# A gated DeltaNet whose triangular solve on GpSimd goes from 16x16 to 32x32 blocks

## What is computed

```python
    decay = jnp.exp(jnp.where(lower, g[..., :, None] - g[..., None, :], -jnp.inf))
    a = jnp.where(strict, jnp.einsum('nbhcd,nbhsd->nbhcs', k_beta, k) * decay, 0.0)
    eye = jnp.eye(DN_CHUNK, dtype=q.dtype)
    t_inv = lax.linalg.triangular_solve(a + eye, jnp.broadcast_to(eye, a.shape),
                                        left_side=True, lower=True, unit_diagonal=True)
    u = jnp.einsum('nbhcs,nbhsd->nbhcd', t_inv, v * beta[..., None])
    w = jnp.einsum('nbhcs,nbhsd->nbhcd', t_inv, k_beta * jnp.exp(g)[..., None])
    ...
        v_new = u_c - jnp.einsum('bhcd,bhde->bhce', w_c, state)
        o_c = (jnp.einsum('bhcd,bhde->bhce', q_c * jnp.exp(g_c)[..., None], state)
               + jnp.einsum('bhcs,bhse->bhce', qk_c, v_new))
    ...
    o = _rmsnorm_f32(o, norm_w) * jax.nn.silu(z.astype(jnp.float32).reshape(bsz, seqlen, DN_NV, DN_DV))
    return o.reshape(bsz, seqlen, DN_V_DIM).astype(x.dtype) @ w_out
```

## Time and profile before

| what | us |
|---|---|
| three runs, median (lowest to highest) | 1464.47 (1462.7 to 1466.74) |
| the profiled execution | 1463.22 |
| its span on the core | 1461.4 |
| TensorE busy in it | 1374.9 (94%), 7494 matmul records |
| VectorE, ScalarE, GpSimd busy | 782.5, 364.7, 293.9 |
| mean granted TensorE clock | 0.978 |

### The profile page before, as it was taken

How to read it: one execution, slowest core, us unless ns; L and a number is a source line. 1 busy time by engine, 2 the same in 40 slices (tenths; PEclk the granted TensorE clock), 3 DMA queues, 4 the chain that set the end, 5 groups by cost and what they waited for, 6 DMA issues and landing times. The chain is left out here.

```text
span 1461.4 us, 21006 instructions
## 1 busy us (share of the span) xinstructions
PE 1374.9 (94%) x7494; PEld 823.8 (56%) x7494; DVE 782.5 (54%) x1577; ACT 364.7 (25%) x788; POOL 293.9 (20%) x529
## 2 busy tenths in 40 slices
PE   8899699999999999999899899999999999889996
PEld 5468268576685766857686433336544544533332
DVE  2765465756657566575556543247344544835227
ACT  3322122222222222222222122102332232222110
POOL 2240613325133251332401200021000000200011
PEclk9999899999999999999899999999999999999998
DMA  7367321313213132122524599981021118299983
GB/s 211 112 179 218 89 74 30 102 38 91 67 37 97 34 97 61 41 68 90 140 76 145 187 387 399 399 314 42 23 75 39 41 39 311 107 349 399 399 311 127
DMA packets 173251, 220.90 MB, mean 151 GB/s; under 512 B 57280, under 2 KB 107840, under 8 KB 173184
## 3 DMA queue, kind: packets, MB, share of 16 engines
q1 hardware_dynamic: 141664, 173.65, 35.6%
q10 hardware_dynamic: 26432, 28.32, 5.7%
q0 software_dynamic: 5088, 18.02, 3.4%
HBM read 185.62 MB, written 34.34 MB: 151 GB/s over the span
## 5 line engine op out<-in xcount | busy, mean ns | idle before, releaser
L498 PE MATMUL bank<-xT,wgu 128*128 128x512 f32 x448 | 195.3, 595 | 0.0
L1894 PE MATMUL bank<-wgu,moe_xgT 128*32 128x512 f32 x1536 | 169.8, 594 | 4.3 <-issue 3.9
L498 PEld LDWEIGHTS bank<-xT,wgu 128*128 128x128 f32 x448 | 84.6, 191 | 101.5 <-issue 101.5
L546 PE MATMUL bank<-wd,oT 128*128 128x512 f32 x256 | 122.1, 614 | 1.4 <-issue 1.4
L590 PE MATMUL bank<-wd,xT 128*128 128x256 f32 x512 | 119.8, 380 | 0.0
L1145 DVE SCALAR_TENSOR_TENSOR wgu<-bank,taps,wgu 128x510 f32<-128x510 f32 (+1 forms) x128 | 95.5, 746 | 44.7 <-ACT wgu L785 38.6
L1894 PEld LDWEIGHTS bank<-wgu,moe_xgT 128*32 128x32 f32 x1536 | 50.1, 110 | 105.8 <-issue 95.0
L590 PEld LDWEIGHTS bank<-wd,xT 128*128 128x128 f32 x512 | 95.0, 191 | 11.4
L1917 PE MATMUL bank<-wd,moe_hidT 128*32 128x512 f32 x768 | 87.1, 593 | 7.2 <-issue 4.1
L2161 DVE TENSOR_TENSOR moe_hid<-moe_silu,bank 128x256 f32<-128x256 f32 x24 | 10.1, 421 | 129.7 <-ACT moe_silu L2004 129.7
L546 PEld LDWEIGHTS bank<-wd,oT 128*128 128x128 f32 x256 | 46.9, 197 | 45.7 <-issue 44.7
(11 more groups left out here) (354 smaller groups left out, 2407.0 us busy)
## 6 DMA issues: line engine op xcount, KB each, us to landing
wgu<-moe_w_gate SPq DMA_DIRECT2D x32, 1024.0 KB, 14.3
wgu<-moe_w_up SPq DMA_DIRECT2D x32, 1024.0 KB, 15.6
wd<-moe_w_down SPq DMA_DIRECT2D x32, 1024.0 KB, 15.4
wgu<-dn_w_in SPq DMA_DIRECT2D x32, 512.0 KB, 4.1
slots_x<-gains SPq DMA_DIRECT2D x1, 9984.0 KB, 35.6
wd<-dn_w_in SPq DMA_DIRECT2D x8, 1024.0 KB, 6.0
wd<-dn_w_out ACTq DMA_DIRECT2D x16, 512.0 KB, 4.4
xT<-slots_x ACTq DMA_DIRECT2D x16, 512.0 KB, 8.6
```

Source lines behind the costliest of these rows:

```text
L498: mm = pe.matmul(bank[:], wqkv[:, ct, k], xT[:, k], start=k == 0, stop=k == KD - 1)
L546: mm = pe.matmul(ps[uses.at[f"{name}{n}"][0]][:], oT[:, h, tt], wo[:, h, half * 512:(half + 1) * 512], start=h == 0, stop=h == 1)
L1894: mm = pe.matmul(ps[2][seats].rearrange("p (a f) -> p a f", a=2), xgT[:, j % ROW_BUFS, k, seats], wgu[:, e % RING, :, k], start=k == 0, st ...
```

## The change

BASE becomes 5: GpSimd inverts blocks of 32 x 32, and levels 5 and 6 are left. Each block lies on two partitions: both have all of the scaled block N, and each has one half of the columns of T. The loop goes over k from 31 to 1. The straight and turned results go out with three stores (T_kept counts 48), the unturned halves in rows of 16 numbers. `take_blocks` has four stores and four loads, `place_solved` and `place_half` two DMAs each. The output scales stand in the middle of the solve (`midway`, behind k = 16). ScalarE clears `forms` in its window, so GpSimd has no memsets in the loop. On TensorE two output products (six in the last head) stand ahead of the first level. VectorE's fourth convolution stands in the window with the others. SP issues the loads of beta, and the zero fill stands behind the blocks of head 1.

```diff
-LEVELS, BASE = 7, 4
+LEVELS, BASE = 7, 5
...
-OUTPUT_EARLY, OUTPUT_LATE = [(f"y{n}", 0) for n in range(4)], [(f"y{n}", n % 2) for n in range(4, 8)]
+OUTPUT_EARLY, OUTPUT_LATE = [("y0", 0), ("y1", 2), ("y2", 0), ("y3", 1)], [(f"y{n}", n % 2) for n in range(4, 8)]
...
-        scaled = sb("scaled", [P, BLK, BLK])
-        raw_blk, S = sb("raw_blk", [P, BLK, BLK]), sb("S", [P, BLK, BLK])
-        prod = sb("prod", [P, 64])
-        T_blk = sb("T_blk", [P, 2, BLK, BLK])
+        HALF = BLK // 2
+        raw_blk = X.rearrange("p c t n -> p (c t n)").rearrange("p (r c) -> p r c", r=BLK)
+        N = W.rearrange("p c t n -> p (c t n)").rearrange("p (r c) -> p r c", r=BLK)
+        T = sb("T", [P, BLK, HALF])
+        T_turned = sb("T_turned", [P, HALF, BLK])
+        prod = sb("prod", [P, HALF * HALF])
...
                 for d in range(2):
-                    sp.dma_start(raw_blk[d * 64:d * 64 + 64].rearrange("p r c -> p (r c)"), t["A_rows"]).then_inc(blocks_in, 16)
+                    for half in range(2):
+                        sp.dma_start(raw_blk[d * 64 + half:d * 64 + 64:2].rearrange("p r c -> p (r c)"), t["A_rows"]).then_inc(blocks_in, 16)
 
             def place_solved(n):
 
                 sp.wait_ge(T_solved, n + 1)
-                sp.dma_start(t["T_rows"].rearrange("f q n -> q f n"), T_blk[:].rearrange("p f r c -> p f (r c)")).then_inc(T_kept, 16)
-                sp.wait_ge(T_kept, (n + 1) * 16)
+                sp.dma_start(t["T_rows"][0], T_turned[:].rearrange("p c r -> p (c r)")).then_inc(T_kept, 16)
+                by_half = t["T_rows"][1].rearrange("(q a) (r c) -> q (a r c)", a=2, c=BLK).rearrange("q (r a c) -> a q r c", a=2, c=HALF)
+                for half in range(2):
+                    sp.dma_start(by_half[half], T[half:P:2]).then_inc(T_kept, 16)
+                sp.wait_ge(T_kept, (n + 1) * 48)
                 sp.wait_ge(forms_zero, n + 1)
                 for b in range(P // BLK // 2):
                     place_blocks(sp, b)
...
             load_w(1, True)
             load_spans(1)
             solve_blocks(0)
-            sp.wait_ge(zeroed, 1)
-            sp.dma_start(t["router_w"], dram["router_w"].rearrange("(k p) e -> p k e", p=P)).then_inc(t["router_in"], 16)
-            sp.dma_start(t["router_b"][:], dram["router_bias"].partition_broadcast(P)).then_inc(t["router_in"], 16)
-
-            for rows, n in ((t["slots_x"], BLOCKS), (t["slots_y"][FETCHED * P:], 1)):
-                blocks = rows.rearrange("(b p) n -> p b n", p=CAP)
-                sp.dma_start(blocks, zeros.rearrange("p (a n) -> p a n", a=1).to_broadcast([CAP, n, D])).then_inc(zero_filled, 16)
             load_w(2, True)
             load_spans(2)
             solve_blocks(1)
             load_z(1, True)
+            sp.wait_ge(zeroed, 1)
+            sp.dma_start(t["router_w"], dram["router_w"].rearrange("(k p) e -> p k e", p=P)).then_inc(t["router_in"], 16)
+            sp.dma_start(t["router_b"][:], dram["router_bias"].partition_broadcast(P)).then_inc(t["router_in"], 16)
+            for rows, n in ((t["slots_x"], BLOCKS), (t["slots_y"][FETCHED * P:], 1)):
+                blocks = rows.rearrange("(b p) n -> p b n", p=CAP)
+                sp.dma_start(blocks, zeros.rearrange("p (a n) -> p a n", a=1).to_broadcast([CAP, n, D])).then_inc(zero_filled, 16)
...
-                if not following:
+                if following:
+                    filler(2)
+                else:
                     pe.wait_ge(cols_in, 64)
                     pe.wait_ge(*last_read(uses, 2, i))
                     pe.matmul(ps[2][:, 0:4 * KD], cols[:], ident[0:4 * KD, 0:4 * KD], start=True, stop=True).then_inc(cols_turned, 1)
-                    filler(4)
+                    filler(6)
...
-                act.wait_ge(T_kept, (n + 1) * 16)
+                act.wait_ge(T_kept, (n + 1) * 48)
                 act.wait_ge(forms_zero, n + 1)
                 for b in range(P // BLK // 2, P // BLK):
                     place_blocks(act, b)
+
+            def clear_forms(f):
+                act.wait_ge(rows_in, 16)
+                for d in range(2):
+                    ins = act.copy(forms[:, f, d].rearrange("p h t n -> p (h t n)"), zero_col.to_broadcast([P, 8 * P]))
+                if f:
+                    ins.then_inc(forms_zero, 1)
...
             def window(uses, i, n):
                 middle_tap(uses, i, n, 0)
+                if uses is not FIRST_HEAD:
+                    clear_forms(0)
                 for ct in range(1, 4):
                     middle_tap(uses, i, n, ct)
                     act_silu(n, ct - 1)
+                    if ct == 1 and uses is not FIRST_HEAD:
+                        clear_forms(1)
                     if ct == 2:
                         place_half(n - 1)
...
+                pool.wait_ge(blocks_in, (i + 1) * 64)
                 for d in range(2):
                     some = slice(64 * d, 64 * (d + 1))
                     raw = raw_blk[some].rearrange("p r c -> p c r") if d else raw_blk[some]
-                    step(nc.gpsimd.tensor_tensor(S[some], raw, scaled[some], ALU.mult))
-                step(nc.gpsimd.tensor_tensor(S[:].rearrange("p r c -> p (r c)")[:, 0:BLK * BLK:BLK + 1], ones[:, 0:BLK], ones[:, 0:BLK], ALU.mult))
-                for k in range(BLK - 2, 0, -1):
-                    n = BLK - 1 - k
+                    step(nc.gpsimd.tensor_tensor(N[some], raw, over_cols[some], ALU.mult))
+                for k in range(BLK - 1, 0, -1):
+                    lo = max(0, k - HALF)
+                    n = HALF - lo
                     part = prod[:, 0:k * n].rearrange("p (r c) -> p r c", r=k)
-                    step(nc.gpsimd.tensor_tensor(part, S[:, 0:k, k:k + 1].to_broadcast([P, k, n]), S[:, k:k + 1, k + 1:].to_broadcast([P, k, n]), ALU.mult))
-                    step(nc.gpsimd.tensor_tensor(S[:, 0:k, k + 1:], S[:, 0:k, k + 1:], part, ALU.add))
-                nc.gpsimd.tensor_tensor(T_blk[:, 1], S[:], over_cols, ALU.mult)
-                nc.gpsimd.tensor_tensor(T_blk[:, 0], S[:].rearrange("p r c -> p c r"), over_rows, ALU.mult).then_inc(T_solved, 1)
+                    step(nc.gpsimd.tensor_tensor(part, N[:, 0:k, k:k + 1].to_broadcast([P, k, n]), T[:, k:k + 1, lo:].to_broadcast([P, k, n]), ALU.mult))
+                    step(nc.gpsimd.tensor_tensor(T[:, 0:k, lo:], T[:, 0:k, lo:], part, ALU.subtract))
+                    if k == HALF:
+                        midway()
+                step(nc.gpsimd.tensor_tensor(T_turned[:], T[:].rearrange("p r c -> p c r"), over_turned, ALU.mult))
+                nc.gpsimd.tensor_tensor(T[:], T[:], over_rows, ALU.mult).then_inc(T_solved, 1)
...
+                def output_scales():
+                    for n in range(2):
+                        pool.wait_ge(oss_ready, 1 + i * 2 + n + 1)
+                        rsqrt(nc, t, pool, rs[:, 4 * n:4 * n + 4], ss[:, 4 * n:4 * n + 4], C_EPS_O, rs_added, i * 2 + n + 1).then_inc(rs_ready, 1)
+
                 if following:
                     key_scales(i + 1)
-                    solve(i + 1)
-                for n in range(2):
-                    pool.wait_ge(oss_ready, 1 + i * 2 + n + 1)
-                    rsqrt(nc, t, pool, rs[:, 4 * n:4 * n + 4], ss[:, 4 * n:4 * n + 4], C_EPS_O, rs_added, i * 2 + n + 1).then_inc(rs_ready, 1)
-                if following:
-                    clear_forms()
+                    solve(i + 1, output_scales)
+                    pool.wait_ge(o_step, 1 + (i + 1) * 8)
                     decayed_scores(i + 1)
+                else:
+                    output_scales()
...
-                for ct in range(3):
...
-                    for slot, job in enumerate(taps_apart(None, i, i + 1, 3)):
-                        jobs[slot] = [job]
-                    jobs[4] = [lambda: silu(i + 1, 2)]
-                    jobs[8] = [lambda: silu(i + 1, 3)]
+                    jobs[2] = [lambda: silu(i + 1, 3)]
                 if earlier:
-                    for n, slot in enumerate((3, 5, 7, 9)):
-                        jobs.setdefault(slot, []).append(lambda n=n: add_output("y", n if following else 4 + n))
+                    for n, slot in zip((1, 0, 2, 3), (0, 1, 4, 5)) if following else ((6, 4), (7, 5)):
+                        jobs.setdefault(slot, []).append(lambda n=n: add_output("y", n))
                 if not following:
-                    jobs["window"] = [lambda: weight_rows()] + [lambda n=n: add_output("y", n) for n in range(4)]
+                    jobs["window"] = [lambda: weight_rows()] + [lambda n=n: add_output("y", n) for n in range(6)]
```

More of the change, by code:

```diff
@@ L41 @@
 C_ROW = C_HALF + 40
-C_SEAT = C_ROW + BLK * BLK
+C_SEAT = C_ROW + 2 * 16
 CAP = 96
@@ L411, in _ @@
             load_z(0, False)
+            sp.wait_ge(beta_kept, 16)
+            for h in range(2):
+                for d in range(2):
+                    by_block = t["beta_rows"][d * NV:(d + 1) * NV].rearrange("(n h) (b j) -> h b n j", h=2, j=BLK)
+                    for half in range(2):
```

(40 more changed lines are left out.)

21 lines of the change are left out of this document (10 added, 11 removed).

## The result

The changed kernel takes 1550.7 us (median of four runs, 1547.9 to 1557.0). The kernel before took 1463.6 on the same chip: the ratio is 1.0582, 95% interval 1.0551 to 1.0614. The profiled execution has a span of 1547.9 us and a mean granted clock of 0.942; before it was 1461.4 and 0.978. The prediction was 1520, 1482 to 1558, slower. Its sign, its range and its mechanism held, and its value was 31 us short.

A forecast was written before the change was run, and what follows sets the result against it. TensorE bounds the kernel before; after the change the blocks' path, 68.4 us against 62.9 of cover, sets the head. Accumulated X delays reach +64 at head 7, less 7.3 behind it: +57 on 1463.2 gives 1520 us, range 1482 to 1558.

The forecast's parts named there:

- Head 0's X product: First X product of head 0 at 123.8 us against 91.62, +32.2, with nothing to cover the longer solve.
- Heads 3 to 6: Steady heads: 92.5 us each, 1.6 more than before.
- the ways out: From solved blocks to X product: 5.6 us to store T and 5.2 us to load forms.
- I add 1.0 us: Second half of GpSimd's solve: VectorE's scans running beside it lengthen it by 1.0 us.
- Head 1 to head 2, the fill: Zero fill delays head 2's blocks to 63.2 us after its issue; head 2's X product at 328.4 us, +47.0.
- Head 6 to head 7: Head 7, with no projections behind its scores: 89.8 us behind head 6, against 79.29 before.
- The cover: Steady head: the blocks' path of 68.4 us exceeds its cover of 62.9, so the X product waits about 5.5 us.
- The first rival: Solve stays under cover through less GpSimd time per element; TensorE remains the bound and the kernel ends faster; 5%.
- The second: Rival: solve 4 to 7 us shorter than taken, heads 3 to 6 at about 85.6 us, kernel 1464 to 1480; 7%.
- the third: Rival: the small stores of T pace the path, 8 us more in each of eight heads, kernel 1586 us; 6%.
- at no cost: ScalarE's clears of forms, the fourth convolution in the window and the beta loads on SP were claimed to add no time.
- The clock's 1.5 us a head: TensorE's low clock behind each pause ahead of the levels: 1.5 us a head, between 0 and 2.9.

The follow-up runs named there:

- experiment 5: Changed kernel with the zero fill issued under head 0's solve and VectorE's four scans moved behind the masks of the scores: 1508.3 us, 1.0277 of the kernel before.
- experiment 2: Changed kernel with the router loads and zero fill issued while head 0 is being solved: 1525.2 us, 1.0416 of the kernel before.
- experiment 1: Changed kernel with GpSimd's loop stopped behind k = 16, so T is not the inverse: 1516.0 us, 1.0347 of the kernel before.
- experiment 4: Changed kernel with the unturned halves of T stored as whole 2 KB rows, not 64 byte pieces: 1954 us, not comparable because TensorE has more records.
- experiment 3: Changed kernel with six unused TensorE products in the wait for forms, in bodies 1 to 6: 1545.5 us, 1.0552 of the kernel before.
- experiment 8: Changed kernel with half the solve loop (T not the inverse), scans moved behind the score masks, fill in five-block pieces: 1477.7 us, 1.0080 of the kernel before.

## Why the prediction was right, and where it was 30 us short

In spans, the sum said +57 and the trace has +86.5. By its own steps, as measured less predicted:

- **Head 0's X product:** +33.2 against +32.2. The solve alone took 43.7 us against 42.6; the wait is 34.66 against 33. Right: 1.9 ns an element carries to the larger tiles. Of the 1.1 too much, 0.85 stand in two instructions of the loop beside VectorE's L1189, whose two inputs are in SBUF.
- **Head 0 to head 1:** 91.1 us against 86.9, 4.2 more. **Heads 3 to 6:** 96.7 against 92.5, 4.2 more in each, 16.8 together. In a steady head the blocks came 1.4 us sooner behind the scores than the 11.4 taken, the ways out took 0.5 more (11.3 against 10.8), X to scores 0.8 more (24.9 against 24.1), and the solve 4.2 more (50.4 against 46.2). This is the term that was mis-sized: "I add 1.0 us" for VectorE's scans beside the solve. Measured against the fastest instruction of each size, what stands beside VectorE's instructions with their inputs in SBUF took 5.4 us more in a steady solve: 3.5 beside the scans (experiment 5 gave back 3.0) and 1.8 beside others, for which the prediction had nothing. Without them the solve would be 45.1, where the same sum without the scans was 45.2.
- **Head 1 to head 2, the fill:** 124.0 against 117.7, 6.3 more: 3.5 by the solve (49.7 against 46.2), 2.3 because the fill started with head 1's X product and not 2.5 us ahead of it (the blocks came 63.1 us behind its issue, 63.2 were predicted), the rest in the ways out. The mechanism and its place were right, and experiment 2 gave its whole price, 25.5 us.
- **Head 6 to head 7:** 93.2 against 89.8, 3.4 more. **Behind it:** 9.0 less against 7.3 less.

These make 1.0 + 4.2 + 16.8 + 6.3 + 3.4 - 1.7 = 30.0 us. The solve is 27.4 of it: 1.1 in head 0, 4.2 in head 1, 3.5 in head 2, 4.2 in each of heads 3 to 6 and 1.8 in head 7 (47.0 against 45.2), and nearly all of that is the work beside VectorE. Head 7 has the scales but no scans beside its solve, so 50.4 - 47.0 = 3.4 us is what the scans cost the others.

**Why 1.0 us was too little.** It came from four qkd products that took 6.22 us beside scans and 5.40 without. But in the kernel before, the scans were over early in that row, which starts at 261.02:

```profile
258.12 5.59 DVE L1122 TENSOR_TENSOR_SCAN wgu<-wgu 128x512 f32<-128x512 f32 x4
```

They end at 263.6, so they ran beside 2.6 of the 6.22 us only. In experiment 1, where the four products (L1051) start at 394.58 and the scans last until 402.1, the products took 8.60 us. The price was read from a row that overlaps in part, and taken as that of a whole overlap.

**The cover.** That the path and not TensorE would set the head held: the X products of heads 0 to 6 end a wait on the DMA of forms, 34.66 us in head 0 and 5.3 to 5.5 in the others (33 and some 5 predicted). Head 7's waits 14.33 us, which the profile puts down to no engine or DMA, but it too stands 11.2 us behind the end of its solve. The first rival, a solve under cover, needed 39 us in each; it was 50. The second is out by the same number, the third by the stores' 5.3 us and experiment 4. The parts moved "at no cost" were so only while the solve was longer: experiment 1 shows the clears 8 us late for a solve of 31.5 (forms was loaded 13.2 us behind it, and the stores take 5.3), and the first convolution's wait growing to 3.90. The clock's 1.5 us a head is what experiment 3 gave back.

**What the upper bound stood on.** The range ended at 1558 for a solve of 46 us at the highest rate and a clock term of 2.9. The time came near it by another term, the work beside the solve, for which I had given a value and no bound. That the range held is in part luck: the room left for the rate and the clock, which were both right, was taken by something else. The lower end doesn't follow from its own terms: 4 us less in each of eight heads and half of the fill's 26.7 us are 45 less, 1475 and not 1482.

## What to carry to other kernels

When a step moves from an engine that bounds the kernel to an idle one, compare the new length of the serial path with its cover, head by head, before counting what the bounding engine saves: here 5.35 us of TensorE were paid with 37 us of path, and 3 us of the solve above its cover were 17 us of the kernel (experiment 5). Price a lengthened step beside its new neighbours, not only by itself, and from rows that overlap with such a neighbour all the time. A large transfer in a shared queue is cheap where the next small load has cover and dear just ahead of a small one that hasn't; cut it into pieces, put each behind the last load that someone waits for, and try that on the kernel before first.

## What the runs showed of the hardware

**GpSimd beside VectorE.** An element-wise instruction of GpSimd on 208 to 224 elements took 1.36 to 1.46 us beside a TENSOR_TENSOR_SCAN, and 0.56 to 0.66 without; a scan of 512 took 1.14 us alone (4.56 for four), 1.5 beside this loop and 2.1 in experiment 1 (8.50 for four). Next to other VectorE instructions with two inputs in SBUF (L1189, L1323, L1378) it took 0.33 to 0.59 us more, as the one at 397.93. In all nine traces with blocks of 32 the slow instructions of the loop are only those beside such work; no run moved it away, other than the scans. VectorE's operations with one input in PSUM, as the one at 410.66 on `bank`, did not slow it. The scan reads two operands in SBUF. GPSIMD Engine Reference of the Trainium skill, Specifications, says that GpSimd shares SBUF interfaces with VectorE and contends with its instructions with two SBUF inputs; these rows agree, and a factor of more than two is the price here.

**A fill holds both queues.** Behind the 10 MB fill, SP's own small issue took 25.59 us, and ScalarE's load, issued on another queue just behind the fill, landed some 43 us later (experiment 1). A piece of five blocks did the same for 3.6 us (experiment 8).
